# Picking one tile instead of two by TensorE ahead of the experts, and loading all four weight slots during the first block's routing

## The chip, the cores and the metric

The kernel runs on one core of one Trainium2 chip. A core has five engines that run side by side: TensorE (PE, matrix products and transposes), VectorE (DVE), ScalarE (ACT), GpSimd (POOL) and SyncE (SP), and 16 DMA engines that move data between HBM and the on-chip memory. The metric is the device time of one execution in microseconds (us), the median of several runs. The profile is one execution recorded by the hardware profiler.

## What is computed

Two transformer blocks on 512 tokens of width 1024. What matters here is the mixture of experts at the end of each block. In the first block it is

```
for e in range(N_EXPERTS):                       # 16
    hid = jax.nn.silu(h @ w_gate[e]) * (h @ w_up[e])
    y = y + gates[..., e:e + 1] * (hid @ w_down[e])
```

Two experts per token have a gate that is not zero. The second block does the same with 32 experts. The inner width of an expert is 256, so the weights of one expert are 2 MB (gate and up) and 1 MB (down), in float32.

## The kernel before, in words

Each block ends with two stages, and each stage is a group of programs, one for each engine, with a barrier of all engines at its end: nothing of the next stage begins before the last engine is through.

**Routing** (`route`, line 1795 on). VectorE works out which two experts each token goes to and the place of each token in its expert's list, and TensorE helps with counts (`totals`, `rbank`). The tokens of an expert form a tile of at most S rows (S is 96 in the first block, 64 in the second). Tile t belongs to expert t as long as no expert has more tokens than S. `tok_of` says which token stands in which row of which tile. It comes last, from the 16 products of line 1886, and then the rows of any tile can be fetched from `token_rows` in HBM. For tiles 0 and 1 the kernel does not wait for that: `first_oh` (line 1949) is a one-hot matrix that follows from `rbank` alone, and `pick_rows(i)` multiplies it with the token rows, which still lie on the chip (`x_res` in the first block, `gates` in the second). The products land in `pick` and are the turned rows of tile i. ScalarE copies them into `first_xT[i]` (line 1903). `pick_rows(0)` stands before the products for `tok_of`, `pick_rows(1)` behind them. SP meanwhile issues loads of weights (`rest_of_loads`).

**Experts** (`experts` in the first block, `experts_moving` in the second). There is a ring of weight slots: 4 in the first block, 7 in the second. In tile t TensorE computes gate and up (the tiles `e_gate` and `e_up` in the first block, `e_gu` in the second), turns the rows of tile t + 1 (`turn_x`, into `e_xbank`; VectorE and ScalarE copy them to `r_xT`, half each), multiplies the hidden values of tile t - 1 with the down weights (`down`, into `e_ybank`), and in the first block computes up only after that. The rows of tile t (`r_xg`) come by an indirect DMA that GpSimd issues, from tile 2 on; it waits only until `r_xg`, which has two buffers, is free. In the first block ScalarE and VectorE also split the down weights into a high and a low part (`xT_hi`, `xT_lo`, lines 2270 and 2217). SP reloads a slot's gate and up weights when tile t's up is done (`gu_done`) and its down weights when these were read. SP's instructions stand in one order: a load that waits holds back all loads behind it. In the second block the load of tile 7's down weights waits for `y_done` of tile 0.

In the first block slots 0 to 2 are loaded before or during the routing, and slot 3 at the head of the experts' stage. After the experts the rows are gathered, added and normed, and the next stages follow.

Of the kernel before, what the change touches and what calls it, by code (L numbers as in the profile page):

```python
# [21 lines left out]
P = 128  # L22
# [1770 lines left out]
def route(k, name, E, G, S, lg, ctx, loads, retired, row_tile):  # L1793
# [14 lines left out]
    k.first_xT = [k.sb(ctx, f"{name}_xT{i}", [P, KD * S]) for i in range(2)]  # L1808
# [11 lines left out]
    with ExitStack() as s:  # L1820
# [14 lines left out]
        first_rank = k.sb(s, f"{name}_first_rank", [P, TT, 2])  # L1835
        first_oh = k.sb(s, f"{name}_first_oh", [P, 2, TT, S])
# [3 lines left out]
        pick = [[k.ps(s, f"{name}_pick{i}{h}") for h in range(2)] for i in range(2)]  # L1840
# [4 lines left out]
        with nc.Block() as block:  # L1845
# [14 lines left out]
            def _(pe):  # L1860
# [10 lines left out]
                def pick_rows(i):  # L1871
                    pe.wait_ge(first_ready, i + 1)
                    for c in range(KD):
                        at = (c % PER * GROUPS + c // PER) * S
                        for tt in range(TT):
                            ins = halves(pe, pick[i][at // XH][:, at % XH:at % XH + S], row_tile(tt)[:, c * P:(c + 1) * P],
                                         first_oh[:, i, tt, :], tt == 0, tt == TT - 1)
                    ins.then_inc(picked_x, 1)

                pick_rows(0)  # L1880
# [8 lines left out]
                pick_rows(1)  # L1889

            @block.scalar
            def _(act):
# [7 lines left out]
                for i in range(2):  # L1900
                    act.wait_ge(picked_x, i + 1)
                    for h in range(2):
                        act.activation(k.first_xT[i][:, h * XH:(h + 1) * XH], pick[i][h][:, 0:XH], ACT.Copy).then_inc(
                            xT_ready, 1)

            @block.vector
            def _(dve):
# [39 lines left out]
                step(dve.scalar_tensor_tensor(first_rank[:], ranks[:, :, 0:2], 1.0, M[:, :, 0:2], ALU.add, ALU.mult))  # L1947
                for i in range(2):
                    dve.tensor_tensor(first_oh[:, i], bc(k.c("iota")[:, 1:S + 1], 1, TT), bc(first_rank[:, :, i], 2, S),
                                      ALU.is_equal).then_inc(first_ready, 1)  # L1950
# [68 lines left out]
def experts(k, name, E, S, x_in, rows, w_gu, w_dn, out_rows, weights, late, tail):  # L2019
# [7 lines left out]
    with ExitStack() as s:  # L2027
        xg = k.xg
        idx = [k.sb(s, f"{name}_idx{i}", [S, 1], U32) for i in range(2)]
        xT = k.first_xT  # L2030
# [52 lines left out]
        with nc.Block() as block:  # L2083
# [48 lines left out]
            def _(pe):  # L2132
                used = pe.value_load(k.used[0:1, 0:1], min_val=E, max_val=NT)

                def turn_x(t, b, n):

                    pe.wait_ge(x_in[b % 2], 16 * n)
# [1386 lines left out]
```

## Time and profile before

| what | value |
|---|---|
| median of 3 runs | 1459.01 us (1456.79 to 1459.05) |
| the profiled execution, whole | 1457.84 us |
| its span in the trace | 1455.9 us |
| TensorE busy | 1248.0 us (86%) |
| VectorE, ScalarE, GpSimd busy | 701.6, 463.3, 418.7 us |
| first block's routing, experts | about 300 to 323 us, 323 to 481 us |
| second block's routing, experts | about 1179 to 1199 us, 1199 to 1431 us |

Times in the trace count from the start of the span; 1.94 us of the execution lie outside of it. In a line of the timeline the first number is the start, the second the length, then engine, line of the code, operation and tiles; in square brackets stands how long the engine was idle before it and what ended that. "SPq" is the issue of a DMA, not its transfer. "PEclk" is the share of TensorE's full clock that was granted.

### The profile page before, as it was taken

Reading aid. Unit: us, or ns where it says so; the run is one execution under the profiler, and the core shown is the slowest. Engines: PE = TensorE matmul, PEld = TensorE weight load, DVE = VectorE, ACT = ScalarE, POOL = GpSimd, SP = SyncE. Lnnn points to the kernel's source line nnn. Section 1 sums busy time; section 2 is a strip of 40 time slices with the busy share of each in tenths; the row PEclk is TensorE's granted clock in tenths of the full one; section 3 lists DMA queues with packets and bytes.
Section 4 is the critical chain, followed back from the end, with each engine's and each line's share of the span. In section 5 each row is a group of like instructions: output and inputs, shape, how many; then the busy total and the mean of one; then the engine's idle time right before and its main releaser. Section 6 shows DMA issues by size and latency. Waiting matters only on the chain. (4 is left out here: it accounts for less than half of the span.)

```text
span 1455.9 us, 25454 instructions
## 1 busy us (share of the span) xinstructions
PE 1248.0 (86%) x10212; PEld 959.7 (66%) x10216; DVE 701.6 (48%) x1273; ACT 463.3 (32%) x1015; POOL 418.7 (29%) x354
## 2 busy tenths in 40 slices
PE   7998768969999159899999999999788969997871
PEld 6776446868887148758979978778676855553430
DVE  5797783554444555662754637682124352111112
ACT  4533243233333244442342243423222321121110
POOL 5354311211110214212414234234334302332223
PEclk9998979989999669999999999999999989999996
DMA  7300183159996603101121313322122499999985
GB/s 273 105 11 1 52 296 148 44 195 359 372 387 260 214 7 129 60 2 65 58 89 62 112 34 113 118 87 66 51 85 93 195 408 412 417 419 420 420 371 186
DMA packets 64918, 261.97 MB, mean 180 GB/s; under 512 B 8226, under 2 KB 18082, under 8 KB 52000
## 3 DMA queue, kind: packets, MB, share of 16 engines
q1 hardware_dynamic: 54176, 233.73, 42.2%
q0 software_dynamic: 8832, 20.36, 4.0%
q10 hardware_dynamic: 1792, 6.29, 1.2%
q8 instruction: 76, 1.25, 0.4%
q14 instruction: 42, 0.34, 0.1%
HBM read 240.73 MB, written 29.43 MB: 186 GB/s over the span
## 5 line engine op out<-in xcount | busy, mean ns | idle before, releaser
L1712 POOL TENSOR_TENSOR block_w_lo<-block_w,block_w_hi 128x512 fp32r<-128x512 f32 x96 | 130.2, 1358 | 210.0 <-ACT block_w_hi L1690 210.0
L2432 PE MATMUL e_gu<-e_w,r_xT 128*64 128x256 f32 x896 | 104.6, 387 | 18.9 <-DMA e_w<-in_gu 17.0
L251 PE MATMUL dil_bank<-block_w_hi,xT_hi 128*128 128x512 f32 x288 | 116.3, 404 | 4.4 <-PEq L842 4.4
L1690 ACT ACTIVATE block_w_hi<-block_w 128x512 fp32r<-128x512 f32 x96 | 60.4, 631 | 178.4 <-PE dil_bank L253 114.5
L253 PE MATMUL dil_bank<-block_w_hi,xT_lo 128*128 128x512 f32 x288 | 114.4, 397 | 0.0
L252 PE MATMUL dil_bank<-block_w_lo,xT_hi 128*128 128x512 f32 x288 | 114.3, 397 | 0.0
L2432 PEld LDWEIGHTS e_gu<-e_w,r_xT 128*64 128x64 f32 x896 | 63.0, 138 | 51.9 <-DMA e_w<-in_gu 19.1
L251 PEld LDWEIGHTS dil_bank<-block_w_hi,xT_hi 128*128 128x128 f32 x288 | 77.9, 270 | 8.5 <-issue 4.7
L252 PEld LDWEIGHTS dil_bank<-block_w_lo,xT_hi 128*128 128x128 f32 x288 | 78.1, 271 | 3.8
L253 PEld LDWEIGHTS dil_bank<-block_w_hi,xT_lo 128*128 128x128 f32 x288 | 77.7, 270 | 3.9
L2494 DVE TENSOR_TENSOR e_prod<-e_sg,e_gu 128x128 f32<-128x128 f32 x32 | 9.2, 288 | 137.5 <-ACT e_sg L2526 137.5
L3161 DVE COPY dil_nat<-dil_bank 128x512 f32<-128x512 f32 x36 | 24.9, 691 | 86.0 <-PE dil_bank L253 84.7
L2392 POOL DMA_INDIRECT r_xg<-token_rows,r_tok_of x30 | 30.6, 1019 | 115.6 <-PE e_xbank L2423 94.5
L2453 PE MATMUL e_ybank<-e_w,e_hT 128*64 128x512 f32 x256 | 62.2, 604 | 0.4 <-issue 0.4
L852 POOL TENSOR_TENSOR block_w_lo<-block_w,block_w_hi 128x512 fp32r<-128x512 f32 x20 | 24.8, 1275 | 124.7 <-ACT block_w_hi L927 124.7
L2152 PE MATMUL e_gate<-r_xT,e_w 128*64 128x96 f32 x1024 | 48.4, 256 | 7.4 <-DMA e_w<-in_gu 3.2
L2217 DVE TENSOR_TENSOR xT_lo<-e_w,xT_hi 128x2048 fp32r<-128x2048 f32 x16 | 36.7, 2293 | 34.0 <-ACT xT_hi L2270 34.0
L2152 PEld LDWEIGHTS e_gate<-r_xT,e_w 128*64 128x64 f32 x1024 | 46.1, 144 | 8.5 <-issue 8.5
L2385 POOL DMA_INDIRECT slot_rows<-e_y,r_y_of x32 | 32.3, 1010 | 65.3 <-ACT e_y L2520 51.2
L251 PE MATMUL gates_bank<-block_w_hi,xT_hi 128*128 128x512 f32 x128 | 49.9, 390 | 1.1 <-PEq L842 1.1
L2526 ACT ACTIVATE e_sg<-e_gu 128x128 f32<-128x128 f32 x32 | 8.9, 277 | 129.3 <-PE e_gu L2432 129.3
L253 PE MATMUL gates_bank<-block_w_hi,xT_lo 128*128 128x512 f32 x128 | 49.8, 389 | 0.0
(512 smaller groups left out, 3071.1 us busy)
## 6 DMA issues: line engine op xcount, KB each, us to landing
e_w<-in_gu SPq DMA_DIRECT2D x44, 2048.0 KB, 27.0
e_w<-in_dn SPq DMA_DIRECT2D x48, 1024.0 KB, 28.1
block_w<-in_w_dil SPq DMA_DIRECT2D x9, 2048.0 KB, 8.1
block_w<-in_w_out SPq DMA_DIRECT2D x4, 2048.0 KB, 9.2
block_w<-in_w_gates SPq DMA_DIRECT2D x4, 2048.0 KB, 11.0
w_t<-in_w_in_t SPq DMA_DIRECT2D x12, 512.0 KB, 3.7
slot_rows<-blank SPq DMA_DIRECT2D x12, 512.0 KB, 5.9
slot_rows<-e_y ACTq DMA_DIRECT2D x16, 384.0 KB, 9.7
```

Of the source, the lines that this page charges most:

```text
L251: pe.matmul(out, lhs[0], rhs[0], start=first, stop=False)
L252: pe.matmul(out, lhs[0], rhs[1], start=False, stop=False)
L253: return pe.matmul(out, lhs[1], rhs[0], start=False, stop=last)
L1690: act.activation(wh[:, j % RING, 0:width[i]], k.w[:, slot, c, 0:width[i]], ACT.Copy).then_inc(hi_ready, 1)
L1712: pool.tensor_tensor(wl[:, j % RING, 0:width[i]], k.w[:, (q0 + i) % 2, c, 0:width[i]], wh[:, j % RING, 0:width[i]].bitcast(F32), ALU.subtr ...
L2152: ins = pe.matmul(bank[b % 2][g * HD:(g + 1) * HD, m * S:(m + 1) * S], w1[b][:, w:w + HD], xT[b % 2][:, c * S:(c + 1) * S], start=(c == 0) ...
L2217: dve.tensor_tensor(w2_part(k.xl, b, 0), w2[b][:].rearrange("p (q n) -> p q n", q=4), w2_part(k.xh, b, 0).bitcast(F32), ALU.subtract).then ...
L2385: pool.indirect_dma_start(halves, bass.IndirectOffsetOnAxis(ap=k.y_of[:, t:t + 1], axis=0), y[t % 2][:], None, bounds_check=GROUPS * SLOTS ...
L2392: pool.indirect_dma_start(xg[t % 2][:], None, parts, bass.IndirectOffsetOnAxis(ap=k.tok_of[:, t:t + 1], axis=0), bounds_check=GROUPS * SEQ ...
L2432: ins = pe.matmul(gubank[t % 2][g * S:(g + 1) * S, 0:2 * FG], xT[t % 2][:, turned_at(c):turned_at(c) + S], w1_piece(slot.of[t], w, 2 * FG) ...
L2453: ins = pe.matmul(ybank[t % 2][m * S:(m + 1) * S, :], hT[:, c * S:(c + 1) * S], w2[b][:, c * DM + m * 512:c * DM + (m + 1) * 512], start=( ...
L3161: return dve.tensor_copy(nat[:, i, tt, :], bank[:, 0:512])
```

## The change

In both routings `pick_rows(1)` goes, with its one-hot matrix, its two banks and the two copies by ScalarE. `first_oh` covers tile 0 alone. In both experts' stages GpSimd starts with a gather of tile 1's rows by `tok_of[:, 1:2]`, and TensorE turns them inside tile 0: behind tile 0's up in the first block, behind tile 0's `e_gu` in the second. VectorE and ScalarE copy them as for every other tile. In the first block the loads of slot 3 (2 MB and 1 MB) move from the head of the experts' stage to the end of `rest_of_loads`. Its core:

```diff
@@ route
-                pick_rows(0)
+                pe.wait_ge(first_ready, 1)
+                for c in range(KD):
+                    ...
+                ins.then_inc(picked_x, 1)
                 for j in range(2 * TT):
...
                 ins.then_inc(tok_done, 1)
-                pick_rows(1)
...
-                for i in range(2):
-                    act.wait_ge(picked_x, i + 1)
-                    for h in range(2):
-                        act.activation(k.first_xT[i][:, h * XH:(h + 1) * XH], pick[i][h][:, 0:XH], ACT.Copy).then_inc(
-                            xT_ready, 1)
+                act.wait_ge(picked_x, 1)
+                for h in range(2):
+                    act.activation(k.xT[0][:, h * XH:(h + 1) * XH], pick[h][:, 0:XH], ACT.Copy).then_inc(xT_ready, 1)
@@ experts
-                first_loads(sp, weights, late, w_gu, w_dn)
                 tail.load(sp)
...
+                pool.indirect_dma_start(xg[1][:], None, rows, bass.IndirectOffsetOnAxis(
+                    ap=k.tok_of[:, 1:2], axis=0), bounds_check=SEQ - 1, oob_is_err=False).then_inc(x_in[1], 16)
                 every_tile(pool, used, tile)
...
                     half(t, b, ubank, FF // P, gu_done)
+                    if isinstance(t, int) and t == 0:
+                        turn_x(1, 1, 0)
...
-                    if not isinstance(t, int) or t >= 1:
-                        with more(t + 1):
-                            copy_x(t + 1, b + 1)
+                    with more(t + 1):
+                        copy_x(t + 1, b + 1)
@@ experts_moving
+                pool.indirect_dma_start(xg[1][:], None, parts, bass.IndirectOffsetOnAxis(
+                    ap=k.tok_of[:, 1:2], axis=0), bounds_check=GROUPS * SEQ - 1, oob_is_err=False).then_inc(x_in[1], 16)
...
                     gate_up(t)
-                    if more is not None and t >= 1:
+                    if more is not None:
                         with more(t + 1):
                             turn_x(t + 1)
@@ first_block
-            first_loads(sp, weights, range(2, 3), d["gu1"], d["dn1"])
+            first_loads(sp, weights, range(2, W_SLOTS), d["gu1"], d["dn1"])
```

TensorE in the first block, from the picking of tile 0's rows to tile 1's gate, before; `e_w_0` and `e_w_1` are the weights of slots 0 and 1, `x_res` the token rows:

```order
L245 MATMUL r_pick<-r_first_oh,x_res 64x96 x64
L1886 MATMUL r_tbank<-r_ohj,r_ohr 96x26 x8
L245 MATMUL r_pick<-r_first_oh,x_res 64x96 x64
L1845 UNCONDITIONAL_BRANCH
L2131 UNCONDITIONAL_BRANCH
L2133 TENSOR_LOAD r_used
L2133 ISA x2
L2152 MATMUL e_gate<-r_xT,e_w_0 64x96 x32
L2152 MATMUL e_up<-r_xT,e_w_0 64x96 x32
L2152 MATMUL e_gate<-r_xT,e_w_1 64x96 x32
L2142 MATMUL e_xbank<-consts,r_xg 128x96 x8
```

The same place in the changed kernel:

```order
L245 MATMUL r_pick<-r_first_oh,x_res 64x96 x64
L1883 MATMUL r_tbank<-r_ohj,r_ohr 96x26 x8
L1845 UNCONDITIONAL_BRANCH
L2125 UNCONDITIONAL_BRANCH
L2127 TENSOR_LOAD r_used
L2127 ISA x2
L2146 MATMUL e_gate<-r_xT,e_w_0 64x96 x32
L2146 MATMUL e_up<-r_xT,e_w_0 64x96 x32
L2136 MATMUL e_xbank<-consts,r_xg 128x96 x8
L2146 MATMUL e_gate<-r_xT,e_w_1 64x96 x32
L2136 MATMUL e_xbank<-consts,r_xg 128x96 x8
```

The second picking is gone, and a turning of tile 1's rows stands between the up of tile 0 and the gate of tile 1.

TensorE at the head of the second block's experts, before; `e_hbank` is the turning of the hidden values, `e_ybank` the down product:

```order
L2432 MATMUL e_gu<-e_w_0,r_xT 64x256 x16
L2441 MATMUL e_hbank<-consts,e_prod 128x128
L2432 MATMUL e_gu<-e_w_1,r_xT 64x256 x16
L2423 MATMUL e_xbank<-consts,r_xg 128x128 x4
L2453 MATMUL e_ybank<-e_w_0,e_hT 64x512 x4
```

And in the changed kernel:

```order
L2427 MATMUL e_gu<-e_w_0,r_xT 64x256 x16
L2418 MATMUL e_xbank<-consts,r_xg 128x128 x4
L2436 MATMUL e_hbank<-consts,e_prod 128x128
L2427 MATMUL e_gu<-e_w_1,r_xT 64x256 x16
L2418 MATMUL e_xbank<-consts,r_xg 128x128 x4
L2448 MATMUL e_ybank<-e_w_0,e_hT 64x512 x4
```

The turning of tile 1's rows stands between tile 0's `e_gu` and everything else of tiles 0 and 1.

SP in the first block, from the routing's loads to the head of the experts' stage, before; `in_gu` are gate and up weights, `in_dn` the down weights:

```order
L3442 DMA e_w_01<-in_dn 128x2048 x2
L1789 DMA e_w_2<-in_gu 128x4096
L1790 DMA e_w_2<-in_dn 128x2048
L1845 UNCONDITIONAL_BRANCH
L2084 UNCONDITIONAL_BRANCH
L2086 TENSOR_LOAD r_used
L2086 ISA x2
L1789 DMA e_w_3<-in_gu 128x4096
L1790 DMA e_w_3<-in_dn 128x2048
L2596 DMA ln_vecs<-in_vecs 128x1024 x2
```

And in the changed kernel:

```order
L3437 DMA e_w_01<-in_dn 128x2048 x2
L1789 DMA e_w_2<-in_gu 128x4096
L1790 DMA e_w_2<-in_dn 128x2048
L1789 DMA e_w_3<-in_gu 128x4096
L1790 DMA e_w_3<-in_dn 128x2048
L1845 UNCONDITIONAL_BRANCH
L2077 UNCONDITIONAL_BRANCH
L2079 TENSOR_LOAD r_used
L2079 ISA x2
L2591 DMA ln_vecs<-in_vecs 128x1024 x2
```

Slot 3's two loads now stand ahead of the barrier, in the routing.

## Rows read from the trace of the kernel before

**Rows 1.** The page: the chain that ended last, by line.
```profile
DMA e_w<-in_gu 8%; PE e_gu L2432 4%; PE e_ybank L2453 2%; DMA e_w<-slot_rows,r_slot 1%; PE e_xbank L2423 1%; POOL e_w L2558 0%; PE e_hbank L2441 0%; DMA slot_rows<-e_y,r_y_of 0%; DVE x_res L2567 0%; POOLq L2351 0%; ACT e_y L2520 0%; DVEq L2482 0%; DVE e_prod L2494 0%; ACT e_sg L2526 0%; POOLq L2328 0%
```

**Rows 2.** The timeline, first block's routing, its last steps.
```profile
306.40 7.59 PE L245 MATMUL r_pick<-r_first_oh,x_res 128*64 128x96 f32 x128 [0.96 <-DVE r_first_oh L1949]
...
315.39 5.50 PE L245 MATMUL r_pick<-r_first_oh,x_res 128*64 128x96 f32 x128
315.57 0.18 DVE L1979 TENSOR_SCALAR r_tok_of<-r_tbank 96x26 uint32<-96x26 f32 x1 [2.63 <-PE r_tbank L1886]
...
320.93 0.87 ACT L1903 ACTIVATE r_xT<-r_pick 128x384 f32<-128x384 f32 x2 [6.03 <-PE r_pick L245]
```

**Rows 3.** Busy times by window; last three columns PEclk, DMA share, GB/s.
```profile
315.00:320.00 5.00, 5.00 (x118) 4.96 (x119) 0.18 (x1) 0.00 (x0) 0.00 (x0) 1.00 0.02 7
...
404.00:413.00 9.00, 8.65 (x139) 7.27 (x136) 3.62 (x6) 3.33 (x4) 1.16 (x2) 1.00 1.02 372
```

**Rows 4.** The timeline, first block's experts, tiles 0 and 1.
```profile
323.16 4.25 PE L2152 MATMUL e_gate<-r_xT,e_w 128*64 128x96 f32 x64 [2.27 <-DVEq L2192]
...
328.32 1.90 ACT L2270 ACTIVATE xT_hi<-e_w 128x2048 fp32r<-128x2048 f32 x1
...
330.12 2.84 PE L2152 MATMUL e_gate<-r_xT,e_w 128*64 128x96 f32 x64
...
333.14 0.36 DVE L2227 TENSOR_TENSOR e_hT_lo<-e_prod,e_hT_hi 128x192 fp32r<-128x192 f32 x1
...
334.51 0.85 PE L2142 MATMUL e_xbank<-consts,r_xg 96*128 96x96 f32 x8 [1.56 <-DMA r_xg<-token_rows,e_idx]
...
335.15 0.45 PE L251 MATMUL e_ybank<-xT_hi,e_hT_hi 128*96 128x512 f32 x1
...
335.40 0.56 DVE L2202 COPY r_xT<-e_xbank 128x384 f32<-128x384 f32 x1 [1.90 <-PE e_xbank L2142]
```

**Rows 5.** The timeline of SP: loads issued when tiles 0, 1 and 7 are through.
```profile
330.50 0.35 SPq L2091 DMA_DIRECT2D e_w<-in_gu  x1
...
341.15 0.33 SPq L2091 DMA_DIRECT2D e_w<-in_gu  x1
...
395.27 0.33 SPq L2091 DMA_DIRECT2D e_w<-in_gu  x1
```

**Rows 6.** The timeline of PE: tile 10's gate, and tile 15's up.
```profile
416.15 4.51 PE L2152 MATMUL e_gate<-r_xT,e_w 128*64 128x96 f32 x64 [1.97 <-DMA e_w<-in_gu]
...
471.77 2.86 PE L2152 MATMUL e_up<-r_xT,e_w 128*64 128x96 f32 x64
```

**Rows 7.** DMA issues at 436.25 (tile 15's gate and up); last column us to landing.
```profile
e_w<-in_gu SPq DMA_DIRECT2D x1, 2048.0 KB, 29.1
```

**Rows 8.** Gathers by line L2121, first block's experts.
```profile
DMA to landing us min/median/max: 10.1/11.2/12.0
```

**Rows 9.** Gathers by line L2392, second block's experts.
```profile
DMA to landing us min/median/max: 7.1/8.1/9.7
```

**Rows 10.** The page, DMA issues: gathers of `slot_rows`, with no weights in flight.
```profile
e_w<-slot_rows,r_slot POOLq DMA_INDIRECT x16, 5.6
```

**Rows 11.** The timeline, second block, end of the routing and head of the experts.
```profile
1193.97 3.92 PE L245 MATMUL r_pick<-r_first_oh,gates 128*64 128x64 f32 x128
...
1199.46 0.98 SPq L3360 DMA_DIRECT2D e_w<-in_dn  x2
...
1200.39 1.07 POOL L2392 DMA_INDIRECT r_xg<-token_rows,r_tok_of  x1 [15.07 <-PEq L2414]
...
1204.39 3.67 PE L2432 MATMUL e_gu<-e_w,r_xT 128*64 128x256 f32 x32
...
1210.58 0.33 SPq L2363 DMA_DIRECT2D e_w<-in_dn  x1
```

**Rows 12.** Busy times by window, around the second block's barrier and behind it.
```profile
1198.00:1203.00 5.00, 3.23 (x30) 2.65 (x32) 3.02 (x12) 1.88 (x3) 2.08 (x2) 1.00 0.85 321
...
1240.00:1280.00 40.00, 40.00 (x281) 20.15 (x279) 6.60 (x20) 7.94 (x20) 13.20 (x13) 1.00 1.01 418
```

More of the change, by code:

```diff
@@ L1807, in route @@
     PER, XH = KD // GROUPS, KD * S // 2
-    k.first_xT = [k.sb(ctx, f"{name}_xT{i}", [P, KD * S]) for i in range(2)]
+    k.xT = [k.sb(ctx, f"{name}_xT{i}", [P, KD * S]) for i in range(2)]
     k.xg = [k.sb(ctx, f"{name}_xg{i}", [GROUPS * S, DM // GROUPS]) for i in range(2)]
@@ L1834, in route @@
         pos, q, over, own = (k.sb(s, f"{name}_{n}", [P, 2, TT]) for n in ("pos", "q", "over", "own"))
-        first_rank = k.sb(s, f"{name}_first_rank", [P, TT, 2])
-        first_oh = k.sb(s, f"{name}_first_oh", [P, 2, TT, S])
+        first_rank = k.sb(s, f"{name}_first_rank", [P, TT])
+        first_oh = k.sb(s, f"{name}_first_oh", [P, TT, S])
         ohr = k.sb(s, f"{name}_ohr", [P, 2, TT, S])
@@ L1839, in route @@
         rbank, totals, tbank = (k.ps(s, f"{name}_{n}") for n in ("rbank", "totals", "tbank"))
-        pick = [[k.ps(s, f"{name}_pick{i}{h}") for h in range(2)] for i in range(2)]
+        pick = [k.ps(s, f"{name}_pick{h}") for h in range(2)]
         (step_d, diff_ready, exp_ready, m_ready, rank_done, oh_ready, tok_done, bits_ready, xg_ready, first_ready, picked_x,
@@ L1869, in _ @@
                 ins.then_inc(rank_done, 1)
[L1871 to L1878, printed above, removed]
-                pick_rows(0)
+                pe.wait_ge(first_ready, 1)
+                for c in range(KD):
+                    at = (c % PER * GROUPS + c // PER) * S
+                    for tt in range(TT):
+                        ins = halves(pe, pick[at // XH][:, at % XH:at % XH + S], row_tile(tt)[:, c * P:(c + 1) * P],
+                                     first_oh[:, tt, :], tt == 0, tt == TT - 1)
+                ins.then_inc(picked_x, 1)
                 for j in range(2 * TT):
@@ L1946, in _ @@
                 ranks = rbank[:, 0:TT * E].rearrange("p (t e) -> p t e", e=E)
[L1947 to L1950, printed above, removed]
+                step(dve.scalar_tensor_tensor(first_rank[:], ranks[:, :, 0], 1.0, M[:, :, 0], ALU.add, ALU.mult))
+                dve.tensor_tensor(first_oh[:], bc(k.c("iota")[:, 1:S + 1], 1, TT), bc(first_rank[:], 2, S),
+                                  ALU.is_equal).then_inc(first_ready, 1)
                 step(dve.tensor_tensor(above[:], bc(totals[:, 0:E], 2, J), bc(full[:], 1, E), ALU.is_gt))
@@ L2016, in __call__, with experts @@
         return self.eng.If(self.used > t)
-def experts(k, name, E, S, x_in, rows, w_gu, w_dn, out_rows, weights, late, tail):
+def experts(k, name, E, S, x_in, rows, w_gu, w_dn, out_rows, weights, tail):
     nc = k.nc
@@ L2263, in tile @@
                     act.activation(sg[:], gbank[b % 2][:, 0:2 * S], ACT.Silu).then_inc(silu_ready, 1)
-                    if not isinstance(t, int) or t >= 1:
-                        with more(t + 1):
-                            copy_x(t + 1, b + 1)
+                    with more(t + 1):
+                        copy_x(t + 1, b + 1)
                     act.wait_ge(w2_in[b], 16 * i + 16)
@@ L2494, in tile @@
                     dve.tensor_tensor(prod[:], sg[:], gubank[t % 2][0:U, FG:2 * FG], ALU.mult).then_inc(prod_ready, 1)
-                    if more is not None and t >= 1:
+                    if more is not None:
                         with more(t + 1):
@@ L2526, in tile @@
                     act.activation(sg[:], gubank[t % 2][0:U, 0:FG], ACT.Silu).then_inc(silu_ready, 1)
-                    if more is not None and t >= 1:
+                    if more is not None:
                         with more(t + 1):
@@ L3442, in rest_of_loads @@
                 sp.dma_start(w2[e], d["dn1"][e]).then_inc(w2_in[e], 16)
[L3443 removed]
+            first_loads(sp, weights, range(2, W_SLOTS), d["gu1"], d["dn1"])
         route(k, "r1", E1, G1, S1, lg, s, rest_of_loads, retired, lambda tt: k.x1[:, tt, :])
         experts(k, "e1", E1, S1, k.gather_sems[0:2], d["rows"], d["gu1"], d["dn1"], d["slots"][0:SLOTS1, :], weights,
[L3447 removed]
+                CombineAndNorm(k, "c1", d["slots"][0:SLOTS1, :], rows_room, ALPHA, vecs,
                                                   mla_chunks(d)[0:2]))
```

22 lines of the change are left out of this document (10 added, 12 removed).

## The prediction

> **What bounds the kernel now.** I read the chain that ended last first: it runs through TensorE and the weight loads of the second block's experts [rows 1]. The reader is to see that the end hangs on DMA there: from the barrier on, the DMA engines move 418 GB/s at a share of 1.01 [rows 12], and 32 experts of 3.15 MB are 100.7 MB, 241 us of such traffic. So time is won or lost there only by moving the start of that traffic or by letting the engines run dry in it. Then come the stretches that the diff touches. In the first block's routing TensorE does the two pickings, and the DMA engines stand at a share of 0.02 during the second [rows 2, 3]. In the first block's experts TensorE starts at 323.16 [rows 4]; its tiles follow each other by (395.27 - 341.15) / 6 = 9.02 us up to tile 7 [rows 5]. Fourteen tiles after 341.15 at that pace would end at 467.4, but tile 15's up ends at 474.63 [rows 6]. The missing 7.2 us begin with waits for weights: tile 10 waited 1.97 us, and its gate then took 4.51 us instead of 2.84 [rows 4, 6]. There the DMA engines are at a share of 1.02 and 372 GB/s [rows 3]; the last weights took 29.1 us to land, against 27 us of three tiles [rows 7]. So the first block's experts are bound by TensorE at first and by DMA volume at the end.
>
> **Part 1: the second picking goes, first block.** 5.50 us of TensorE, and the copies of 0.87 behind it [rows 2]. The stage ended with the copies at 321.80, and TensorE started 1.36 us later. Now the last is `tok_of`, which ends at 315.75 [rows 2], so TensorE starts tile 0 at about 317.1: **6.0 us earlier**. VectorE's second `first_oh` goes too; the first picking hides it.
>
> **Part 2: tile 1's rows come by a gather, first block.** Its issue comes about 0.9 us after the stage's first load in the second block [rows 11]; I take 317.8. TensorE is through with tile 0 in 330.12 - 323.16 = 6.96 us [rows 4], at 324.1. From then the price is the landing, L us after issue, plus turning and copy, from 334.51 to 335.96, with the step to the product about 1.55 us [rows 4]. All of that was absent before. Bounds of L: 5.6 us with no weights in flight [rows 10], 10.1 to 12.0 in this stage with 4 MB and more queued ahead [rows 8]. In the second block it is 7.1 to 9.7 [rows 9]. With slot 3 loaded earlier only its rest and 1 MB of vectors are in flight, so I take **8**, near the second block's rows. The rows then land at 325.8 and tile 1's gate starts at 327.35, 2.8 us earlier than 330.12.
> Queued behind that wait: ScalarE's copy of tile 1 stands before its split of tile 0's down weights, and VectorE's before its half. That split had been done early, at 328.32; from there to the end of `e_hT_lo` are 5.2 us [rows 4]. Now this chain starts with tile 1's gate, so tile 0's down starts at 327.35 + 5.2 = 332.55, against 335.15 [rows 4]. The old wait of 1.56 us for tile 2's rows [rows 4] goes, since its gather is issued right behind, but the chain takes its place. Should TensorE's clock drop after the wait, as at tile 10 (+1.67 us [rows 6]), this 5.2 us chain hides it too. **Tile 1 ends 2.6 us earlier**, at 338.55. Bounds: L = 5.6 gives 3.7 earlier (TensorE's own tile 0 is then late), L = 12 gives 1.4 later.
>
> **Part 3: slot 3's loads move into the routing.** 3.15 MB at 372 GB/s are 8.5 us of DMA. The earlier loads are through by 314, and from 315 on the engines stood still [rows 3], so these bytes go into a hole. They end near 320 and delay nothing of slots 0 to 2, which stand before them in the queue. SP's two issues are short. In the old stage slot 3, the vectors (1.05 MB) and tile 2's gather all lay before the first reload; now that stream starts with tile 4's weights at the end of tile 0, about as early as slot 3 did. Every later load lands about (3.15 + 1.05 + 0.26) / 0.372 = 12 us earlier, less 1 for the start: tile 15's gate and up at 436.25 + 29.1 - 11 = 454.3 instead of 465.35 [rows 7]. TensorE now asks for them at 338.55 + 13 x 9.02 = 455.8. So the waits just vanish; I leave 0.6 us, since the down weights land some 4 us behind. **6.6 of the 7.2 us go.** Late is next TensorE itself. Bounds: 0 (the lateness isn't volume) and 7.2.
> The first block's sum is -2.6 - 6.6 = -9.2 us, and all stages between the blocks move by that.
>
> **Part 4: second block.** The picking of 3.92 us goes [rows 11], and half a `first_oh` on VectorE, which is the bound there; the stage starts some 4.2 us earlier, SP's first loads at 1195.3 (all times here without the first block's gain). Before, the DMA engines thinned out around the barrier, a share of 0.85 over 5 us, that is 0.75 us lost [rows 12]. That goes. But TensorE now waits in tile 0 for a gather issued at 1196.2: with L = 7.6 it lands at 1203.8, then 1.3 us for turning and copy, 3.67 for tile 1's `e_gu` [rows 11], 0.7 for turning tile 2's rows and 1.9 for tile 0's down: `y_done` of tile 0 at 1211.4, against the old reload at 1210.58 [rows 11]. With a clock drop in the 4.4 us wait, as at tile 10, it is 1213.0. SP's reload of tile 7's down weights waits for it, and tile 8's gate and up stand behind. The queue holds by then, from 1199.5 on, 2.9 MB of slots 5 and 6, tile 7's 2.1 MB and two gathers: 5.3 MB, 12.6 us at 418 GB/s, empty near 1212. A load's data starts 1 to 2 us after its issue. So the engines run thin for 0 to 2.5 us; I take 1.5. Net **+0.8 us**, bounds -0.75 (no thinning) and +2.9 (L = 9.7 adds 2.1; the end of the DMA stream moves one for one).
> The Trainium skill, DMA: Bandwidth & Descriptors, section Anatomy of one DMA — SWDGE (gpsimd) path, puts a DMA issued by GpSimd at about 2.0 us plus its bytes by 436 GB/s; an estimate by it is 2.6 us for the gather of tile 1. The traces' shortest is 5.6 us. By that rule TensorE would wait in neither block, which is the first rival below.
>
> **Sum:** -9.2 + 0.8 = -8.4 us. The profiled execution took 1457.84 us (span 1455.9) and becomes 1449.4 (span 1447.5). It lies 1.2 us below the median of the runs, so the forecast for the median is 1459.01 - 8.4 = **1450.6 us**.
>
> **Rivals.** *Gathers that land quickly.* L of 5.6 or less in both blocks: 3.7 us instead of 2.6 in tile 1, no thinning in the second block, -0.75: -3.7 - 6.6 - 0.75 = -11.05, **1448.0**. For it: queues are shorter than in the rows of the experts. Against: weights are still in flight in both places.
> *Slow gathers.* L = 12 in the first block, 9.7 in the second: tile 1 ends 1.4 us later, and since TensorE then asks for weights later, all 7.2 go, +2.9 in the second: 1.4 - 7.2 + 2.9 = -2.9, **1456.1**. For it: the stage's own gathers [rows 8].
> *The tail is not volume.* The weights are late because of a slow DMA engine among the 16 or the way requests mix, and slot 3's earlier load cures nothing: -2.6 + 0.8 = -1.8, **1457.2**, which is no change. Against: the hole of 5 us and the share of 1.02 [rows 3].
> *Slower: the slowest DMA engine decides.* A gather and a load count only when their last engine is through. If that lag, and not the volume, makes tile 10 wait, it makes tile 1's gather late as well, on TensorE's path in both blocks. Then 1.4 later in the first block, no cure, and +2.9 in the second: +4.3, **1463.3**. It decides, by 0.2%, from L of 10.6 in the first block and 9.7 in the second: -1.8 + 2.6 + 2.1 = 2.9. For it: a reload takes 29.1 us though its bytes are 5.6 us of traffic. Against: the engines are at a share of 1.02 there, so most of it is queue.
>
> **How the numbers follow.** Forecast 0.58, quick gathers 0.14, slow gathers 0.12, uncured tail 0.10, slower 0.06. A measurement of this kernel can tell 0.2%, 2.9 us, from no change. Faster by more, below 1456.1: the forecast, quick gathers, half of the slow ones and a little of the uncured tail, 0.80. Within: 0.14. Slower: 0.06. The range must leave out 0.2 at most: from 1446.5, below the quick gathers, to 1457.0, which takes in the slow gathers and half of the uncured tail.
>
> **What would show it.** TensorE's first gate of the first block's experts at about 317.1. A wait of TensorE on `r_xg` of about 1.7 us before tile 1's gate; tile 0's down at 332 to 333; no gap for weights at tiles 9 to 15 and the last up ending near 465.4; DMA share near 1 until about 320. In the second block (minus 9.2): TensorE idle for some 4 us after the first `e_gu`, SP's reload of down weights 0.5 to 2.5 us later relative to its old place, and a dip of the DMA share there instead of at the barrier. The prediction is wrong if waits for weights stay at tiles 9 to 14, if either gather lands after more than 10 us, or if TensorE's slow clock lasts through tile 1 of the second block and empties the queue for over 3 us.

## The result, and the profile after

| | before | after |
|---|---|---|
| median | 1457.15 us (1452.2 to 1459.45, 20 runs) | 1452.22 us (1448.57 to 1456.19, 20 runs) |
| profiled execution, whole | 1457.84 us | 1449.4 us |
| its span | 1455.9 us | 1447.6 us |

The ratio is 0.9969 (95% interval 0.9959 to 0.998), a gain of 4.5 us (2.9 to 5.9). Here and below a gain is that of the ratio, which goes by all the runs, and not the distance of the two medians (4.9 us here). Single executions that ran disturbed as a whole, at a lower granted clock (2128.79 us in e3, 1672.44 us of the kernel before beside it), are not in the ratios. The changed kernel is faster, inside the range. The two profiled executions lie 8.4 us apart, the forecast sum to the tenth, but the gain is about half of that. The experiments take both halves of this apart: why the sum of the traces came out, and why it was not what the change is worth.

The page of the changed kernel: first the chain that ended last (its parts by engine, as shares of the span), which stands against [rows 1].
```profile
span 1447.6 us, 24974 instructions
...
PE 1244.5 (86%) x9968; PEld 954.4 (66%) x9972; DVE 701.5 (48%) x1273; ACT 462.3 (32%) x1013; POOL 421.3 (29%) x356
...
DMA 10%; PE 6%; POOL 1%; issue 0%; POOLq 0%; DVE 0%; SPq 0%; ACT 0%; DVEq 0%
```
The end still hangs on the weight loads. TensorE is only 3.5 us less busy although 9.4 us of pickings are gone. So most of the 8.4 us between the two executions must be in when it works.

The timeline after, end of the first block's routing and tiles 0 and 1, against [rows 2, 4]:
```profile
314.99 0.18 DVE L1972 TENSOR_SCALAR r_tok_of<-r_tbank 96x26 uint32<-96x26 f32 x1 [3.06 <-PE r_tbank L1883]
...
316.74 4.51 PE L2146 MATMUL e_gate<-r_xT,e_w 128*64 128x96 f32 x64 [1.87 <-DVEq L2187]
317.29 1.14 POOL L2116 DMA_INDIRECT r_xg<-token_rows,r_tok_of  x1 [13.15 <-issue]
...
325.51 0.85 PE L2136 MATMUL e_xbank<-consts,r_xg 96*128 96x96 f32 x8 [1.61 <-DMA r_xg<-token_rows,r_tok_of]
...
326.78 1.90 ACT L2263 ACTIVATE xT_hi<-e_w 128x2048 fp32r<-128x2048 f32 x1
...
327.05 4.51 PE L2146 MATMUL e_gate<-r_xT,e_w 128*64 128x96 f32 x64 [0.70 <-DVE r_xT L2197]
...
332.16 0.45 PE L251 MATMUL e_ybank<-xT_hi,e_hT_hi 128*96 128x512 f32 x1
...
337.79 2.81 PE L2146 MATMUL e_gate<-r_xT,e_w 128*64 128x96 f32 x64
```
TensorE starts tile 0 at 316.74 instead of 323.16, waits 1.61 us for the rows of tile 1, runs tile 1's gate mostly at the lower of its two clocks (4.51 us instead of 2.84), and is 3.0 us ahead of before at tile 2's gate (337.79 against 340.79). Of these, 0.5 us are older than the change: the routing's first load was issued at 299.45 and not at 299.99.

Next a gate and the last up late in the stage against [rows 6], then the landing of tile 15's gate and up weights, issued at 429.02, against [rows 7]:
```profile
410.62 2.81 PE L2146 MATMUL e_gate<-r_xT,e_w 128*64 128x96 f32 x64
...
461.82 2.86 PE L2146 MATMUL e_up<-r_xT,e_w 128*64 128x96 f32 x64
```
```profile
e_w<-in_gu SPq DMA_DIRECT2D x1, 2048.0 KB, 25.0
```
There is no wait for weights left. Tile 10's gate, which had waited 1.97 us and then run at half speed, starts at 410.62. The last up ends at 464.68 (forecast 465.4). The engines that had stood still from 315 to 320 [rows 3] now work (busy times by window; the last three columns are PEclk, DMA share, GB/s):
```profile
315.00:320.00 5.00, 3.26 (x44) 3.29 (x46) 2.31 (x12) 3.53 (x4) 1.80 (x3) 0.70 0.99 419
```

The timeline after, second block, against [rows 11], and behind it the windows around its first reload:
```profile
1184.64 0.81 SPq L3355 DMA_DIRECT2D e_w<-in_dn  x2
...
1185.06 3.67 PE L2427 MATMUL e_gu<-e_w,r_xT 128*64 128x256 f32 x32 [2.14 <-DVEq L2477]
1185.41 1.07 POOL L2398 DMA_INDIRECT r_xg<-token_rows,r_tok_of  x1 [10.99 <-PEq L2409]
...
1192.73 1.12 PE L2418 MATMUL e_xbank<-consts,r_xg 128*128 128x128 f32 x4 [4.00 <-DMA r_xg<-token_rows,r_tok_of]
...
1194.42 5.23 PE L2427 MATMUL e_gu<-e_w,r_xT 128*64 128x256 f32 x32 [0.35 <-DVE r_xT L2483]
...
1202.16 0.33 SPq L2356 DMA_DIRECT2D e_w<-in_dn  x1
```
```profile
1191.00:1196.00 5.00, 2.91 (x13) 2.04 (x15) 0.62 (x2) 0.38 (x1) 1.00 (x1) 0.50 1.01 410
...
1201.00:1203.00 2.00, 2.00 (x14) 0.78 (x12) 0.29 (x1) 0.60 (x1) 1.00 (x1) 1.00 0.64 244
```
TensorE waits 4.00 us for the gather, the granted clock is 0.50 (1.2 of 2.4 GHz) afterwards, and `e_gu` takes 5.23 us instead of 3.67. The reload of tile 7's down weights stands 34.1 us behind the routing's last down load (1168.09), where it stood 31.6 us behind it before. The DMA share dips to 0.64 just around that issue. At the barrier it no longer dips; against [rows 12]:
```profile
1184.00:1189.00 5.00, 3.67 (x32) 2.65 (x32) 3.33 (x13) 1.51 (x2) 2.08 (x2) 1.00 1.01 431
```

### The profile page after: what moved, and what is told of

Read it like the earlier page. It is cut to its first block and busy times, and to the rows that moved or that the text cites. A ratio compares the mean times of both kernels' runs of the same rounds, so it can differ in the third digit from the quotient of the medians.

```text
span 1447.6 us, 24974 instructions
## 1 busy us (share of the span) xinstructions
PE 1244.5 (86%) x9968; PEld 954.4 (66%) x9972; DVE 701.5 (48%) x1273; ACT 462.3 (32%) x1013; POOL 421.3 (29%) x356
## 5 line engine op out<-in xcount | busy, mean ns | idle before, releaser
L2896 POOL TENSOR_TENSOR block_w_lo<-block_w,block_w_hi 128x384 fp32r<-128x384 f32 (+2 forms) x28 | 29.2, 1049 | 71.0 <-ACT block_w_hi L2923 71.0
## 6 DMA issues: line engine op xcount, KB each, us to landing
e_w<-in_gu SPq DMA_DIRECT2D x44, 2048.0 KB, 21.8
block_w<-in_w_gates SPq DMA_DIRECT2D x4, 2048.0 KB, 10.8
```

The costliest lines, as they stand in the source:

```text
L2896: pool.tensor_tensor(wl[:, j % RING, 0:width[i]], k.w[:, (first_chunk + i) % 2, c, 0:width[i]], wh[:, j % RING, 0:width[i]].bitcast(F32), ...
```

## The experiments

To compare traces without the drift ahead of a stretch, I cut each of them at the same events. **A**: from the first down load of the first block's routing to tile 2's gate. **B**: from there to the first load of the next stage, so the rest of the first block's experts. **Middle**: from the load of the positions, some 41 us behind the end of B, to the second routing's last down loads ahead of its barrier (1178.98 in the kernel before); no edit touches this stretch. **D**: from those loads to the last `e_gu`, the stream of weights. **E**: from there to the first store of the output. Outside of the table stand the start up to A (297.2 to 302.4 us), the 40.6 to 41.8 us between B and the middle, and the 14.5 to 15.9 us behind E. All in us; the right column is the time against the runs of before in the same comparison. The stretches of e3 are read from e3_again, a second execution of the same kernel.

| kernel | A | B | middle | D | E | measured |
|---|---|---|---|---|---|---|
| before | 40.80 | 153.44 | 643.05 | 239.68 | 21.38 | 0 |
| before_again | 40.54 | 154.69 | 646.18 | 239.16 | 21.84 | |
| after | 38.34 | 146.42 | 643.02 | 241.29 | 22.65 | -4.5 |
| after_again | 38.57 | 146.24 | 646.17 | 239.80 | 23.10 | -3.5 |
| e1 load only | 38.49 | 145.96 | 647.48 | 239.39 | 21.63 | -7.1 |
| e2 gather only, first block | 41.79 | 146.34 | 643.12 | 239.70 | 21.64 | -3.2 |
| e3_again second block only | 39.60 | 151.69 | 647.78 | 239.88 | 21.61 | +0.4 |
| e4 first block only | 39.15 | 146.38 | 645.43 | 239.21 | 22.21 | -6.5 |
| e5 filled wait | 39.07 | 146.60 | 645.63 | 239.33 | 22.77 | -5.0 |
| e6 reload order | 37.64 | 146.29 | 645.55 | 239.06 | 22.82 | -5.4 |
| e10 split first, filled | 37.75 | 146.97 | 646.16 | 239.21 | 21.80 | -7.1 |
| e12 gather in the routing | 46.16 | 146.03 | 645.75 | 239.48 | 21.38 | +0.6 |
| e13 the same in both blocks | 44.96 | 146.41 | 643.13 | 244.50 | 21.78 | +6.7 |

The middle alone varies by 4.8 us, with no order by kernel: one trace of a kernel, whole, says little about 5 us. The stretches by themselves repeat much better. B above all has two groups of values and nothing between: 151.7 to 154.7 in the three traces whose kernel leaves the first block as it was, 146.0 to 147.0 in all others.

**The parts of the first block, one at a time.** e1 is the kernel before with the loads alone moved:
```diff
-            first_loads(sp, weights, range(2, 3), d["gu1"], d["dn1"])
+            first_loads(sp, weights, range(2, W_SLOTS), d["gu1"], d["dn1"])
...
-                range(3, W_SLOTS), CombineAndNorm(
+                range(0), CombineAndNorm(
```


> The kernel before, with slot 3's two loads moved into the first block's routing and nothing else. My account (the tail of the first block's experts is late by DMA volume): tile 1 ends where it did, the waits for weights at tiles 9 to 15 vanish, the last up ends 7.2 us earlier, total -7.2 us. Rival (the lateness is the lag of a slow DMA engine, and volume ahead changes nothing): waits for weights of 2 us remain, total within 1 us of before.

1448.74 us, ratio 0.9951 (0.9933 to 0.997), **7.1 us faster**: more than the 4.5 us of the whole change, though the two intervals overlap. B is 146.0, so the loads alone cure the late weights. The total is the expected one, but the surprise is A. Both pickings are still there, tile 1 was expected to end where it did, and yet A is 38.49, as short as with the change. A and B together are 9.1 us shorter than in the traces of before, so that the total agrees to the tenth is luck. The timeline of e1, first block's experts:
```profile
324.83 4.52 PE L2154 MATMUL e_gate<-r_xT,e_w 128*64 128x96 f32 x64 [2.32 <-DVEq L2194]
...
325.93 1.16 POOL L2123 DMA_INDIRECT r_xg<-token_rows,e_idx  x1 [1.03 <-issue]
...
331.79 2.84 PE L2154 MATMUL e_gate<-r_xT,e_w 128*64 128x96 f32 x64
...
334.56 0.88 PE L2144 MATMUL e_xbank<-consts,r_xg 96*128 96x96 f32 x8
...
340.83 2.81 PE L2154 MATMUL e_gate<-r_xT,e_w 128*64 128x96 f32 x64
```
The product on tile 2's rows, `e_xbank` at 334.56, follows the gate at once, where the kernel before had waited 1.56 us [rows 4]. The DMA issues say why, tile 2's gather in e1:
```profile
r_xg<-token_rows,e_idx POOLq DMA_INDIRECT x1, 6.4
```
and the same gather in the kernel before, issued right behind slot 3's loads:
```profile
r_xg<-token_rows,e_idx POOLq DMA_INDIRECT x1, 10.1
```
6.4 us against 10.1: with slot 3's 3.15 MB out of its way this gather is in time.

e2 does the other half alone: in the first block the second picking goes and the gather of tile 1 comes, slot 3 stays at the head of the experts' stage. (`PICKS` is the number of tiles that are picked; the experts' edits are those of the change.)
```diff
+    PICKS = 1 if name == "r1" else 2
...
-                pick_rows(1)
+                if PICKS == 2:
+                    pick_rows(1)
```


> The kernel before, with tile 1 gathered in the first block only, slot 3's loads still at the head of the experts' stage, second block as before. My account: the gather now has 4 MB beside it and lands after about 10.5 us, tile 1 ends 0 to 0.5 us earlier; the stream of weights starts 6 us earlier, so most of the tail's waits go: total -5 to -6 us. Rival (only the hole that slot 3 fills counts): tail uncured, total -0.3 us.

1452.75 us, ratio 0.9978 (0.9963 to 0.9992), 3.2 us faster; 5 to 6 were expected, and the rival's 0.3 lies below the interval. The gather now lands 10.7 us after its issue, and TensorE waits 4.26 us for it:
```profile
328.23 1.51 PE L2146 MATMUL e_xbank<-consts,r_xg 96*128 96x96 f32 x8 [4.26 <-DMA r_xg<-token_rows,r_tok_of]
```
A is 1.5 us longer than in the traces of before (mean 40.3), so the picking, 6 us of TensorE's path, buys nothing in A and the wait takes it all back. Yet B is short: the stage, and with it the stream of weights, starts 6 us earlier, slot 3's loads at 316.5 instead of 322.9, while TensorE asks for them later.

e4 has both edits in the first block and leaves the second as it was before.


> The changed kernel with the second block put back as before (two tiles picked there). My account: the first block's whole gain and no loss: -9.5 us, 1.6 us under the changed kernel. Rival (the second block's change is neutral): like the changed kernel, -4.5 to -8.

1450.34 us, ratio 0.9955 (0.9937 to 0.9973), 6.5 us faster, not 9.5. A 39.15 and B 146.38 are e1's within 0.7 us. So the two edits of the first block **don't add up**: each takes the same late weights away, and in A the gather costs what the picking saved. The time lies in the rival's band (4.5 to 8), which doesn't show the rival's reason, a second block that costs nothing.

**The second block.** e3 has the edit of the second block alone (`PICKS = 2 if name == "r1" else 1`).


> The kernel before, with the second block's routing and experts as in the changed kernel, first block as before. My account: TensorE waits 4 us for the gather in tile 0, runs at its lower clock in tile 1, the reload of tile 7's down weights comes 2.5 us later and the DMA queue runs thin there: total +1.6 us (0 to +3). Rival (the second block is not what cost the rest): -0.7 us, the thin stretch at the barrier goes and none comes.

1457.73 us, ratio 1.0003 (0.999 to 1.0017), 0.4 us slower, no change that can be told: the interval reaches from 1.5 us faster to 2.5 slower and holds both the expected +1.6 and the rival's -0.7. The trace is that of a second execution of the same kernel:


> The kernel before with only the second block changed, for a trace. From the routing's last loads to the last e_gu: my account 241.3 us as in the changed kernel, against 239.7 before; rival (the loss there belongs to that one execution): 239.7.

```profile
1205.21 1.12 PE L2427 MATMUL e_xbank<-consts,r_xg 128*128 128x128 f32 x4 [3.89 <-DMA r_xg<-token_rows,r_tok_of]
```
(The timeline of e3_again.) The wait is 3.89 us as in the changed kernel, `e_gu` takes 5.47 us behind it, the reload stands 34.2 us behind the routing's last down loads, and D is 239.88. In its first block, which is as before, the weights are late again, by 0.34, 0.98, 1.05 and 0.70 us at four tiles, without the drop of the clock at tile 10 of [rows 6]. D is 239.88, near the rival's 239.7 and not the 241.3 of my account: the long D of the changed kernel's first trace did not come again. D is 241.29, 239.80 and 239.88 in the three traces of kernels with this edit and no remedy for it, against 239.4 as the mean of the seven that keep the picking (239.16 to 239.70): +0.9 us in the mean, of which one trace gives the most; by the other two it is 0.4 to 0.5. What does come again is the dip around the late reload, in e3_again:
```profile
1213.00:1215.00 2.00, 2.00 (x9) 0.52 (x9) 0.41 (x1) 0.49 (x2) 1.00 (x1) 1.00 0.64 264
```

To see whether the clock or the place of the reload makes the dip, e5 fills the wait with 16 spare products of the identity, whose results nobody uses:
```diff
+                    if t == 1:
+                        for _ in range(16):
+                            pe.matmul(hbank[:, 0:P], k.c("ident"), k.c("ident"), start=True, stop=True)
                     pe.wait_ge(x_in[t % 2], 16 * ((t + 1) // 2))
```


> The changed kernel; while TensorE waits for tile 1's gather in the second block it runs 16 spare products of 128x128 (their result is not used). My account (half of what the second block's stream lost comes from the lower clock in tile 1's first products, half from the wait itself): PEclk stays at 1.00 there, e_gu of tile 1 takes 3.67 us instead of 5.23, the reload of tile 7's down weights comes 1.6 us earlier, the thin stretch of DMA shrinks, and from the routing's last loads to the last tile's e_gu it takes 240 us instead of 241.3. Rival (the wait alone decides): still 241.3.

The timeline of e5, second block:
```profile
1195.08 3.84 PE L2426 MATMUL e_hbank<-consts 128*128 128x128 f32 x32
...
1199.58 0.66 PE L2432 MATMUL e_xbank<-consts,r_xg 128*128 128x128 f32 x4 [0.66 <-DMA r_xg<-token_rows,r_tok_of]
...
1200.80 3.67 PE L2441 MATMUL e_gu<-e_w,r_xT 128*64 128x256 f32 x32 [0.46 <-DVE r_xT L2497]
```
The clock stays up: `e_xbank` takes 0.66 us instead of 1.12, `e_gu` 3.67 instead of 5.23. The reload comes 1.6 us earlier, and D is 239.33 (240 was expected). e6 leaves the wait and takes SP's queue instead: tile 8's gate and up weights are loaded ahead of tile 7's down weights, so that nothing stands behind the late one.
```diff
-                for t in range(R, E):
+                for part in ("gu", "dn"):
+                    for t in (R, R + 1):
+                        load(t, t, part)
+                for t in range(R + 2, E):
                     load(t, t)
```


> The changed kernel; in the second block SP asks for tile 8's gate and up weights before tile 7's down weights, so that this load waits for tile 1's e_gu alone and not for tile 0's down. My account: it is issued 2.5 us earlier (near 13 us after the stage's first load instead of 17.9), the DMA queue does not run thin, and the stretch to the last e_gu is 239.7 us, as before the change. Rival (the stream lost its time elsewhere): still 241.3.

The timeline of SP in e6, tile 8's gate and up weights, 31.5 us behind the routing's down loads instead of 34.4, and behind it the busy times by window around the place where the dip was:
```profile
1204.51 0.33 SPq L2371 DMA_DIRECT2D e_w<-in_gu  x1
```
```profile
1204.00:1206.00 2.00, 2.00 (x16) 0.89 (x13) 0.70 (x2) 0.66 (x2) 0.17 (x1) 1.00 1.06 424
1206.00:1208.00 2.00, 2.00 (x15) 0.82 (x13) 0.29 (x1) 0.60 (x1) 0.83 (x1) 1.00 0.96 393
```
No dip, and D is 239.06. The dip stands in all three traces with the edit and no remedy and in neither of these two, which shows the way that it goes: a late gather, then a late reload, then a thin queue. Both D are again in the range of the kernels that keep the picking; as that range is itself 0.5 us wide, the size of what they give back is less sure than the way. In time they give about a microsecond: e5 is 1452.41 us, ratio 0.9966 (0.9953 to 0.9978), 5.0 us faster than before; e6 1451.83 us, 0.9963 (0.9945 to 0.9981), 5.4 us faster; the intervals overlap with that of the change.

**The wait in the first block.** e10 is e4 with the split of tile 0's down weights ahead of the copy of tile 1's rows on ScalarE and VectorE, and seven spare products in TensorE's wait.
```diff
+                    early = isinstance(t, int) and t == 0
+                    if early:
+                        split()
                     with more(t + 1):
                         copy_x(t + 1, b + 1)
-                    ...
+                    if not early:
+                        split()
```


> The changed kernel with the second block as before; in the first block tile 0's down weights are split before tile 1's rows are copied, and TensorE runs 7 spare products while it waits for tile 1's gather. My account (the gather's wait, the lower clock behind it and the split chain gave back what the second picking had cost): tile 0's down starts 1.4 us earlier behind tile 1's gate, tile 1 ends 1.4 us earlier, total 1.4 us under the same kernel without this, about 3 us better than with the picking kept. Rival (the gather's landing alone decides): tile 1 ends where it did, within 0.3 us.

The timeline of PE in e10:
```profile
326.97 0.85 PE L2149 MATMUL e_xbank<-consts,r_xg 96*128 96x96 f32 x8 [0.89 <-DMA r_xg<-token_rows,r_tok_of]
...
328.52 2.86 PE L2159 MATMUL e_gate<-r_xT,e_w 128*64 128x96 f32 x64 [0.70 <-DVE r_xT L2211]
...
337.57 2.81 PE L2159 MATMUL e_gate<-r_xT,e_w 128*64 128x96 f32 x64
```
Tile 1's gate runs at the full clock (2.86 us), and tile 1 takes 9.05 us instead of 10.74. A is 37.75, 1.4 us less than e4's. But this gather took 9.1 us to land, and the end is the same: 1449.71 us (1448.03 to 1450.62), ratio 0.9951 (0.9935 to 0.9967), 7.1 us faster, as e1. That is 0.6 us under e4 and not the expected 1.4, and nothing under the kernel that keeps the picking, where 3 had been expected.

**The kernels before and after once more**, to see what repeats:


> The kernel before, unchanged, for a second trace of the same code. My account (the profiled execution of before had one more slow-clock stretch, at tile 10, than others): from the first block's first load in the routing to the next stage's first load 191 to 193 us instead of 194.2, as in the one other trace with this first block (191.3). Rival (it is always there): 194.2.

> The changed kernel, unchanged, for a second trace and times beside those of the next two. My account: the first block's stretch 184.8 to 185.7 us, as in all traces with this first block; the second block's stream to the last e_gu 239.9 to 241.3 us, and from there to the output 22.7 us, against 21.7 with the picking kept. Rival (the 1.6 us of the first trace come every time): 241.3.

after_again: 1452.5 us (1449.02 to 1455.78), ratio 0.9976 (0.9959 to 0.9993), 3.5 us faster. before_again took 1459.86 us, with a B of 154.69: weights were late by 1.50, 0.80, 0.36 and 2.19 us. A and B together are 195.2 us, not the expected 191 to 193, so the first trace was no unlucky one. The late weights belong to the kernel before, but where they fall and whether they cost the clock changes between executions.

**The gather earlier still.** If its landing is the price, it might be issued in the routing, as soon as `tok_of` is there, while the stage closes. e12 is e4 with this, and with the split first as in e10.
```diff
                 pool.wait_ge(xg_ready, 2)
+                if name in ('r1',):
+                    pool.wait_ge(tok_ready, 1)
+                    ...
+                    pool.indirect_dma_start(k.xg[1][:], None, src, bass.IndirectOffsetOnAxis(
+                        ap=k.tok_of[:, 1:2], axis=0), ...)
```


> The changed kernel with the second block as before; the gather of tile 1 in the first block is issued inside the routing as soon as tok_of is there, not behind the barrier, and tile 0's down weights are split first. My account (the picking's 5.5 us were given back to the gather's 8 to 9 us of landing): the gather is issued about 1.7 us earlier, TensorE hardly waits before tile 1 and keeps its clock, tile 2's gate starts 36.5 us after the routing's first load instead of 38.3 to 39.2, total 1.5 to 2 us under the same kernel without this. Rival (something else holds tile 1): within 0.5 us.

1456.98 us, ratio 1.0004 (0.9987 to 1.002): the gain is gone. The timeline of e12:
```profile
313.08 0.18 DVE L1988 TENSOR_SCALAR r_tok_of<-r_tbank 96x26 uint32<-96x26 f32 x1 [3.37 <-PE r_tbank L1894]
...
314.34 1.14 POOL L1863 DMA_INDIRECT r_xg<-token_rows,r_tok_of  x1 [12.41 <-issue]
...
322.66 0.81 SPq L2619 DMA_DIRECT2D ln_vecs<-in_vecs  x2
...
322.94 4.15 PE L2163 MATMUL e_gate<-r_xT,e_w 128*64 128x96 f32 x64 [9.96 <-DVEq L2205]
```
Neither theory had this. The next stage begins 8.3 us after the gather's issue, on all engines at once, with TensorE idle for 9.96 us. The gather landed 7.2 us after its issue, 1.1 us before that: the barrier opens behind the landing. SP's loads do not hold it in this way: in the changed kernel the DMA engines were still at a share of 0.99 with them when the experts' stage began at 316.5. e13 does it in both blocks (it is the changed kernel with this and the split first):


> The same with the second block's picking of tile 1 dropped too and its gather issued inside the second routing. My account: TensorE's wait of 4 us in tile 0 shrinks to about 2.2, the reload of tile 7's down weights comes 13 to 14 us after the stage's first load, the stream to the last e_gu takes 239.5 us, and the total is that of the previous kernel within 1 us. Rival (the second block without its second picking always costs): 1.5 to 2 us over it.

1462.47 us, ratio 1.0046 (1.0028 to 1.0065), **6.7 us slower**, where my account had e12's time and the rival 1.5 to 2 us over it. The second block's barrier shows the same, in the timelines of GpSimd and SP:
```profile
1190.61 1.07 POOL L1863 DMA_INDIRECT r_xg<-token_rows,r_tok_of  x1 [9.85 <-DVEq L1992]
...
1199.32 0.81 SPq L3383 DMA_DIRECT2D e_w<-in_dn  x2
```
TensorE is idle for 10.45 us. The gather landed after 7.8 us and the stage began 0.9 us behind that; in e13's first block it was 7.4 and 1.2. D grows by 5.1 us, since there the weight stream itself is what the barrier holds. That it is the landing which opens the barrier is read from these three places; no run tests it by itself.

e1 and e10 beat the kernel before by 7.1 us each, and their middle values lie 2.6 us under that of the changed kernel, with intervals that overlap its own; e1 is the simpler one, the kernel before with two loads moved.

## Why the prediction was right in the sign and half right in the size

**Part 1 held.** Tile 0 starts 17.3 us after the routing's first down load instead of 23.2: 5.9 us earlier, forecast 6.0.

**Part 2 held in its rows and failed in its meaning.** The gather lands after 8.1 us (forecast 8; 8.2 to 9.1 in the five other kernels' traces with both edits), tile 1's gate starts at 327.05 (forecast 327.35), tile 0's down at 332.16 (332.55), and the chain through the split hides the lower clock as forecast: tile 1 takes 10.74 us against 10.67 before. A is shorter by 2.5 us in the first pair, and by 1.8 against the mean of before in the five traces with both edits and nothing more in this place (after, after_again, e4, e5, e6), forecast 2.6. The step that failed is "The old wait of 1.56 us for tile 2's rows [rows 4] goes, since its gather is issued right behind". It goes because slot 3's loads are gone from the queue, and it goes in e1 too, pickings and all. I had priced parts 1 and 2 against the kernel before, with slot 3 still ahead of tile 2's gather; against the kernel with the loads moved they are worth nothing (38.49 in e1, 38.6 in the mean of the five).
The gather of tile 1 took 8.1 us in the first block and 7.3 in the second. The trace has its bytes too, some 0.17 to 0.19 MB and 0.13 MB, less than the 0.26 MB that the prediction took. The Trainium skill's page (DMA: Bandwidth & Descriptors, section Anatomy of one DMA — SWDGE (gpsimd) path), whose rule gave the prediction its estimate of 2.6 us, would give an estimate of 2.4 and 2.3 us for those bytes. The measurement decides: beside a queue of weights that price isn't to be had, and the first rival, quick gathers, fell with it. Two smaller slips of the prediction changed nothing: the 5.6 us of [rows 10] are a median and not the shortest (4.6 us), and by its own steps a quick gather would end tile 1 earlier by 4.3 us and not by 3.7, as TensorE would then wait for its own tile 0 only.

**Part 3 held.** B falls from 153.3 (mean of three) to 146.4 in the same five traces: 6.9 us, forecast 6.6. That it was volume is shown twice: by e1, which moves 3.15 MB into the hole, and by e2, which starts the same stream 6 us earlier. The rival "the tail is not volume" is out, and the slower one with it: it needed a gather of 10.6 us in the first block, and with slot 3 loaded early the gathers took 8.1 to 9.1.

**Part 4 held in its chain.** The wait was 4.0 us (forecast 4.4), the clock fell, the reload came 2.5 us later (forecast 0.5 to 2.5), the dip at the barrier went and one came at the reload. e5 and e6, which each take one link away, leave no dip. The size is less sure: D is +0.9 us as a mean of three, forecast +0.8, but +1.9, +0.4 and +0.5 one by one. The 1 to 2 us from a load's issue to its data had no row; in the trace of before data moved 1.0 us after the issue at 299.99 and 0.6 us after that at 322.88.

**Luck in the two agreements.** The 8.4 us between the two profiled executions are not the sum's terms alone. A, B and D give -7.9 us, E gives +1.3, and the stretches that the change doesn't touch (the start, the 41 us behind B, the middle and the end) happened to give -1.7. In the second pair of traces (before_again and after_again) A, B and D give -9.8, E again +1.3, and the other stretches -2.3, 10.8 us in all. And the median of 1452.22 us lies only 1.6 us above the forecast 1450.6 because the three runs from which the forecast started lay 1.9 us above the median of all twenty.

**What the sum left out.** Two things.
First, E. It is 22.6 to 23.1 us in after, after_again, e5 and e6, against 21.7 as the mean of the seven that keep the second block's picking: +1.1 us, of which the prediction has no word. GpSimd issues its first gather of `slot_rows` later; the timeline of after, and below it that of before:
```profile
1424.27 0.98 POOL L2553 DMA_INDIRECT e_w<-slot_rows,r_slot  x1 [4.41 <-issue]
```
```profile
1432.17 0.98 POOL L2558 DMA_INDIRECT e_w<-slot_rows,r_slot  x1 [3.03 <-POOLq L2408]
```
It sat idle for 4.41 us before it instead of 3.03 (4.3 in e5). What the engines compute ahead of it is not what is late: the last store of `e_y` is issued 9.50 us after the last `e_gu` in every trace and lands 2.9 to 3.7 us later. The gather then follows the landing by 0.9 to 1.0 us in nine traces and by 1.7 to 2.3 in these four, with nothing that the profile shows in between. Yet e3_again and e13 have the second block's edit and an E of 21.6 and 21.8. Why it costs a microsecond in four kernels and none in two isn't settled.
Second, the baseline. The prediction carried a sum that was read from one profiled execution over to the median ("the forecast for the median is 1459.01 - 8.4"). By the table the stretches give -8.7 for the first block, +0.9 for D and +1.1 for E, -6.7 in all, and 4.5 and 3.5 were measured. The sum of A, B, D and E, against the same means, is too good in every kernel, in most of them by about 2 us: e1 -9.2 for -7.1, e2 -5.2 for -3.2, e3 -1.9 for +0.4, e5 -6.9 for -5.0, e10 -9.0 for -7.1, e12 -1.6 for +0.6. It is less in e4 and after (1.2 and 1.5) and more in after_again, e6 and e13 (3.5, 3.5 and 3.7). An offset that all share points at the traces of the kernel before: they took 1457.84 and 1459.86 us where the medians beside them were 1457.15 and 1456.74. Three traces that are late by 5 to 8 us of weights may well be later than the typical run. That is argued, not shown; some 2 us of the forecast 8.4 stay open.

**So the size.** The kernels with the loads moved that keep the second block's picking gain 6.5, 7.1 and 7.1 us; those that drop it gain 3.5, 4.5, 5.0 and 5.4. The loads are the gain, the edit of the first block's picking is neutral on top of them, and that of the second block costs about 2 us beside them. Alone, in e3, it costs 0.4 us (from -1.5 to +2.5), so its price is the least certain of the three. The traces give 0.9 of the 2 us to D and 1.1 to E; e5 and e6, with D repaired, still stand 1.7 us below the first three, which speaks for E as the larger part. If that is so, the forecast of a second block that costs 0.8 us was too kind by E.

## What to carry over

Before two edits of one change are added up, price each on top of the other: here both cured the same late weights, and what the second saved in A its own gather took back, so it was worth nothing. Time taken off an engine's path by replacing its work with a transfer is paid back in the transfer's landing, and that is read from gathers that share the queue with the same bytes (8 us here), not from quiet ones. A load moved into a stretch where the DMA engines stand still was worth more than all TensorE work removed beside it: 7.1 us alone (e1), 4.5 with that work removed too.

## What the runs showed of the hardware

- A gather by GpSimd that is issued inside a stage holds the barrier at its end: in e12 the next stage began 8.3 us after the issue, in e13 8.6 us (first block) and 8.7 us (second block), each time 0.9 to 1.2 us after the landing, though nobody in the stage waits for the rows.
- A gather of a tile of 96 rows landed after 6.4 us behind 1 MB of vectors (e1), 8.1 to 9.1 behind these and the rest of slot 3 (six traces with both edits), and 9.6 to 10.7 behind these and slot 3 as a whole (before, before_again, e3_again, e2).
- After an idle time of 4.00 us the granted clock was 0.50 (1.2 GHz) and `e_gu` took 5.23 us. With 3.84 us of spare products in that wait it took 3.67. The Trainium skill, TensorE: Matmul & The Clock Gate, section Why this matters for your kernels, warns of idle gaps between bursts of products; the rows agree. In e5 products without use kept the granted clock at 1.00.
- The middle, a stretch of 643 to 648 us that no edit touches, varied by 4.8 us between executions.
